# Splitting the neighbourhood attention's outputs: high part by ScalarE from PSUM, low part by VectorE from PSUM

## What is computed

```python
logits = jnp.concatenate([s_loc.reshape(b, h, GRID_W, kh * kw), s_ctx], axis=-1)
p = jax.nn.softmax(logits, axis=-1).astype(v.dtype)
...
return (jnp.einsum('bhqrw,brqwhd->bqhd', p_loc, v_nb)
        + jnp.einsum('bhqk,bkhd->bqhd', p_ctx, v_ctx))
...
y = jnp.concatenate([a_lat.reshape(b, s, NA_WIDTH), g_lat], axis=-1) @ w_out
```

## Time and profile before

| | |
|---|---|
| median of 3 runs | 1070.91 us (1070.49 to 1071.44) |
| the profiled execution's own time | 1070.63 us |
| its span | 1068.9 us |
| TensorE / VectorE / ScalarE / GpSimd busy | 98% / 73% / 54% / 6% |
| granted TensorE clock over the stage of the change | 1.00 |
| stage of the change (steps 0 to 10, then evoA0 to evoA3) | from 499 to 565 us of the span |

### The profile page before, as it was taken

The page is one execution under the profiler, slowest core; times in us unless marked ns, Lnnn a source line. Parts: engine busy times, 40 slices in busy tenths (PEclk is TensorE's granted clock), DMA queues, the critical chain, the costliest instruction groups (busy, mean ns, idle before and its releaser), DMA issues.

```text
span 1068.9 us, 21419 instructions
## 1 busy us (share of the span) xinstructions
PE 1046.1 (98%) x9034; PEld 998.6 (93%) x9034; DVE 781.0 (73%) x1130; ACT 580.9 (54%) x883; POOL 66.6 (6%) x78
## 2 busy tenths in 40 slices
PE   8999999999999999999999999999999999999997
PEld 8989889999999999897688999999899999999996
DVE  6467778765576768987877999967687769677642
ACT  5556666565546665534656655543554457565432
POOL 2000000000010514000100000000010020000000
PEclk9999999999999999999999999999999999999999
DMA  9557657566755675444557888867768666555621
GB/s 283 178 180 254 228 167 220 181 193 180 246 165 163 198 215 158 137 141 162 194 193 242 276 291 272 270 251 288 260 222 285 225 213 207 186 183 180 235 79 40
DMA packets 165915, 220.29 MB, mean 206 GB/s; under 512 B 4497, under 2 KB 146221, under 8 KB 165820
## 3 DMA queue, kind: packets, MB, share of 16 engines
q1 hardware_dynamic: 164442, 215.67, 62.0%
q0 software_dynamic: 832, 1.65, 0.8%
q10 hardware_dynamic: 546, 1.60, 0.4%
HBM read 217.80 MB, written 1.11 MB: 205 GB/s over the span
## 4 chain that ended last, share of the span: by engine, by line
PE 78%; DVE 15%; ACT 3%; issue 2%; DMA 1%; SPq 0%; DVEq 0%; ACTq 0%
PE psG L580 19%; PE psG L582 19%; PE psG L581 19%; DVE wlo L1853 5%; PE psS L580 4%; PE psS L582 4%; PE psS L581 4%; DVE arow L1919 1%; PE psG L701 1%; PE psG L703 1%; DVE sq L2309 1%; PE psG L714 1%; DVE stat L2357 1%; PE psS L868 1%; PE psG L728 1%
## 5 line engine op out<-in xcount | busy, mean ns | idle before, releaser
L1853 DVE TENSOR_TENSOR wlo<-raw,whi 128x1024 fp32r<-128x1024 f32 x311 | 376.8, 1249 | 101.7 <-ACT whi L1264 96.4
L580 PE MATMUL psG<-Hlo,whi 128*128 128x256 f32 x1420 | 404.5, 285 | 2.9 <-DVE wlo L1853 1.4
L582 PE MATMUL psG<-Hhi,whi 128*128 128x256 f32 x1420 | 400.2, 282 | 0.0
L581 PE MATMUL psG<-Hhi,wlo 128*128 128x256 f32 x1420 | 399.9, 282 | 0.0
L1264 ACT CAST whi<-raw 128x1024 fp32r<-128x1024 f32 x311 | 314.2, 1048 | 116.6 <-PE psG L582 30.5
L580 PEld LDWEIGHTS psG<-Hlo,whi 128*128 128x128 f32 x1420 | 268.3, 189 | 6.7 <-issue 3.7
L581 PEld LDWEIGHTS psG<-Hhi,wlo 128*128 128x128 f32 x1420 | 268.4, 189 | 0.0
L582 PEld LDWEIGHTS psG<-Hhi,whi 128*128 128x128 f32 x1420 | 268.4, 189 | 0.0
L580 PE MATMUL psS<-Glo,whi 128*128 128x256 f32 x316 | 89.8, 284 | 0.0
L582 PE MATMUL psS<-Ghi,whi 128*128 128x256 f32 x316 | 89.1, 282 | 0.0
L581 PE MATMUL psS<-Ghi,wlo 128*128 128x256 f32 x316 | 89.1, 282 | 0.0
(11 more groups left out here) (456 smaller groups left out, 1780.0 us busy)
## 6 DMA issues: line engine op xcount, KB each, us to landing
raw<-in_ada_w_dram SPq DMA_DIRECT2D x48, 1024.0 KB, 5.6
raw<-in_ffn_w_up_dram SPq DMA_DIRECT2D x44, 1024.0 KB, 5.2
raw<-in_w_in_dram SPq DMA_DIRECT2D x29, 1024.0 KB, 6.1
raw<-in_ev_w_in_dram SPq DMA_DIRECT2D x26, 1024.0 KB, 5.5
raw<-in_ffn_w_down_dram SPq DMA_DIRECT2D x22, 1024.0 KB, 4.8
raw<-in_od_w_in_dram SPq DMA_DIRECT2D x12, 1024.0 KB, 8.1
raw<-in_w_in_dram SPq DMA_DIRECT2D x9, 512.0 KB, 6.8
raw<-in_w_o_dram SPq DMA_DIRECT2D x4, 1024.0 KB, 5.2
```

The source lines that it names most:

```text
L580: mm(o, a_hi, b_lo, start=first, stop=False, skip_group_check=shared)
L581: mm(o, a_lo, b_hi, start=False, stop=False, skip_group_check=shared)
L582: return mm(o, a_hi, b_hi, start=False, stop=last, skip_group_check=shared)
L1853: V.tensor_tensor(ring_half(wlo, v, h - H0[v]), src, ring_half(whi, v, h - H0[v]).bitcast(F32), ALU.subtract).then_inc(lo_split, 1)
```

## The change

`keep_na(j)` no longer copies to `vt` and no longer casts. A new function `high_na(j)` on ScalarE waits for the pair's two `na_weigh`, writes `Hhi` from `psY` and counts up a new semaphore `na_high`; it stands at steps 5, 7 and 9 behind `keep_turned(s-2, 0)`, and for the last pair behind the loop, ahead of the `whi` casts that follow. VectorE waits for `na_high`, subtracts `Hhi` from `psY` into `Hlo`, which now frees `psY`, and counts up `M_ready`. `keep_na` keeps its places in VectorE's program.

```diff
@@ ScalarE
+            def high_na(j):
+
+                act.wait_ge(yed, NG + 2 * j + 2)
+                nc.scalar.copy(Hhi[:, j, :], psY[:, 0:S]).then_inc(na_high, 1)
+
             for s in range(NA + 2):
                 if s >= 2:
                     keep_turned(s - 2, 0)
+                if s >= 5 and s % 2 == 1:
+                    high_na((s - 5) // 2)
                 if s == 4:
                     ahead(SPAN["hg"][1])
...
                 keep_rows(f"na{s}b")
+
+            high_na(3)
 
             def square_part(i, g):
@@ VectorE
             def keep_na(j):
 
-                dve.wait_ge(yed, NG + 2 * j + 2)
-                then(V.tensor_copy(vt[:, 1, :], psY[:, 0:S]), y_kept, NG + j + 1)
-                split_value(vt[:, 1, :], Hhi[:, j, :], Hlo[:, j, :], M_ready, 3 + j + 1)
+                dve.wait_ge(na_high, j + 1)
+                then(V.tensor_tensor(Hlo[:, j, :], psY[:, 0:S], Hhi[:, j, :].bitcast(F32), ALU.subtract),
+                     y_kept, NG + j + 1)
+                dve.sem_inc(M_ready, 1)
```

More of the change, by code:

```diff
@@ L353, in build @@
         sub_sq, sub_sum, sub_inv = sem("sub_sq"), sem("sub_sum"), sem("sub_inv")
-        M_ready = sem("M_ready")
+        M_ready, na_high = sem("M_ready"), sem("na_high")
         gate_e = sem("gate_e")
```

## The result

The changed kernel takes 1072.57 us in the median of 22 executions (1070.87 to 1074.77), the kernel before 1070.74 (1070.49 to 1071.44, 22 executions). The ratio is 1.0014, 95% interval 1.0008 to 1.0020: slower by some 1.5 us, or by 1.83 us if the two medians are subtracted. That is inside the range of 1069.4 to 1072.8 and within the 0.2% that I called no change, but 1.2 us above the predicted 1071.4, and above the narrower range of 1070.7 to 1072.1 that I gave the forecast itself.

The account below looks back on a forecast made before the run. VectorE was taken to bound steps 5 to 7, and when keep_na may begin to matter in steps 8 to 10. -1.46 + 1.93 = +0.47 us gave 1071.4 us; range 1069.4 to 1072.8, the forecast's own 1070.7 to 1072.1.

Parts of the forecast that it names:

- Step 5: Pair 0: copy and cast go, wlo starts 0.96 us earlier on VectorE, of which TensorE gains only 0.69 us.
- step 7: Pair 1: keep_na shrinks from 1.25 to 0.46 us, so evoB3 and na_weigh(5) come 1.46 us earlier.
- Step 9: Pair 2: high_na(2) queues behind keep_turned(7, 0), so add_gated comes 1.93 us later after na_weigh(5); ada at 548.65.
- the sum: Over the whole run: 1.46 us gained and 1.93 us lost give +0.47 us.
- TensorE waits for the bank, so all 1.93 us lie on the path: At step 9: add_gated frees the bank the ada needs, so its whole 1.93 us delay counts.
- more idle time than 0.77: Sign of being right: the ada of step 9 starts near 548.6 after TensorE idles longer than 0.77 us.
- rival 3: Slower: step 9's queue costs 1.93 us and the earlier gain does not come; 1072.8 us, chance 0.15.
- After the loop: Pair 3: high_na(3) delays the whi casts, but this is hidden and costs nothing; without cover 0.3 to 0.8 us.
- Rival 1: The bank at step 9 does not hold up TensorE's later work, so the 1.46 us remain: 1069.4 us, chance 0.12.
- Rival 2: All of VectorE's saved time over the four pairs counts, 4.4 us: 1066.5 us, chance 0.07.

Follow-up runs that it names:

- warm_gap10: The changed kernel with 10 idle matmuls of ident by ident in TensorE's gap ahead of the ada of step 9: 1071.35 us, ratio 1.0002.
- swap_last: swap_after with high_na(3) moved behind the two whi casts on ScalarE: 1068.66 us, ratio 0.9980.
- high_early: The changed kernel with high_na(2) moved on ScalarE from behind keep_turned(7, 0) to the end of step 8: 1069.07 us, ratio 0.9982.
- before_late: The kernel before with three additions on an idle buffer on VectorE at step 9, ahead of add_gated: 1074.77 us, ratio 1.0035.
- swap_after: The changed kernel with add_gated of evoB3 ahead of keep_na(2) in VectorE's program at step 9: 1068.62 us, ratio 0.9978.

## Why the prediction was right, and what it left out

**Step 5** held: the subtraction at 0.43 us, the multiplications held up by GpSimd and done at 526.32 (524.68 + 1.74 - 0.10), where 526.35 was forecast; `wlo` 0.98 us earlier, forecast 0.96.

**What reached TensorE there was mis-sized.** I let it gain 0.69 us, the idle time shown before evoB1. scores(7) came 0.97 us earlier (533.81 before, 532.84 after once the 0.10 is taken off), all that VectorE had gained. The ends of TensorE's rows are modelled: after, evoB1 starts at 527.91, while the row of the transposition ahead of it runs to 528.12, so the idle time shown is less than what TensorE can gain. In step 7 the step from the subtraction to the next instruction was 0.57 us and not 0.46 (535.65 to 536.22), which took some 0.1 back. So the gain at evoB3 was 1.64 in place of 1.46 us.

**Step 9** held closely, in part because two small errors cancelled: the wait in front of add_gated of 4.09 us (some 4 forecast), and 1.97 us from the old to the new order (0.33 + 1.64), where 1.93 was summed. VectorE started 0.03 us behind the high part where I had 0.1, and needed 0.57 us from there to add_gated where I had 0.46. The `ada` came 0.33 us later; 0.47 was forecast. As a price of the wait alone the +0.47 us of the sum is close to what `warm_gap10` (+0.40) and the faster group of executions (+0.44) show.

**What failed** is "TensorE waits for the bank, so all 1.93 us lie on the path". I priced TensorE's longer idle time as time only. The forecast even named "more idle time than 0.77" as its sign, and never asked what the matmuls behind it would cost. The missing term is the clock, which the sum put at nothing: 2.8 us in the profiled execution, 1.7 us between the medians of the two groups, and by the times in thirteen of 22 executions. Between the medians of the two kernels 0.47 us was forecast and 1.83 measured. That the median still lies in the range is luck: its upper end, 1072.8, came from rival 3 and not from this mechanism. The rows of before, with 0.77 us idle and 1.00 granted in the stage, could not give its price; they could have given the warning that the gap would grow more than threefold.

**After the loop** the forecast of no cost held (`swap_last`), and evoA1 did not wait for `wlo`.

**Rival 1** (the gain is kept) is what `high_early` shows once the queue allows it: -1.78 us. **Rival 2**, all of VectorE's 4.4 us, was never near. **Rival 3** landed close to the median for the wrong reason: it had the early gain fail, and that gain came in full.

What stays open is why some executions with a gap of 2.7 us keep their clock: the times show two groups, but only one execution of each kernel was profiled. The profiles show at least that the fall does not come at one fixed place of the gap. In the changed kernel it came inside the gap (0.95 in 546 to 548, 0.50 from 548, the `ada` at 548.61), in `before_late` only behind the start of the `ada` (551.17; 0.91 in 551 to 552, then 0.50).

## What to carry to other kernels

When work is handed from one in-order engine to another, price the wait, and then list what is queued behind the waiting instruction; moving the one instruction that others wait for ahead of the wait (`swap_after`) was worth 4 us against the changed kernel. The change with its queue mended is worth 1.5 us. If the wait ends up as idle time on TensorE, look at how long that gap becomes, not only at how much later its end is: a gap that grew to 2.7 us was followed by 6 us at half clock in the profiled execution, and by the times more than half of the executions paid for it. A spread that widens from 1 to 4 us between two kernels is a result in itself; look at the single times before the median.

## What was not expected of the hardware

- Around gaps of 2.22, 2.73 and 2.91 us on TensorE the clock fell to 0.50 in the profiled executions; the times of the others say that it fell in some and not in others of the same kernel. With 1.49 us and 0.77 us no time shows it. In the profiled execution of the changed kernel it lasted until past 554 us, although TensorE was busy without a break from 548.61 on.
- 10 small matmuls whose result nobody uses kept the clock at 1.00 in the profiled execution (`warm_gap10`) and took 1.2 us off the median (1072.57 to 1071.35).
- One execution (`before_late`) was granted 0.95 in every stretch where others show 1.00, and its time (1075.24) lay within those of the same kernel.
